# A mixture-of-experts block whose weights are laid out by the host in the order and shape in which the kernel loads them

## The chip, the cores and the metric

The kernel runs on one core of a Trainium2 chip. The metric is the device time of one execution in microseconds, the median of several runs. All data are float32. Weights lie in device memory (HBM) and are loaded into the on-chip memory SBUF (128 partitions) by DMA. The preparation of the inputs on the host is not part of the time.

## The reference

One layer over 256 tokens of width 1024. First an attention part with two branches, then a mixture of 32 experts of which each token uses four:

```
xn = rms_norm(h, attn_norm); proj = xn @ w_in            # 1024 x 4640
o_a = latent attention (8 heads), o_b = differential attention (4 heads)
merged = sigmoid(gate_a) * (o_a @ w_branch_mla) + sigmoid(gate_b) * (o_b @ w_branch_diff)
h = h + merged @ w_out
t = rms_norm(h, ffn_norm)
logits = t @ w_router + b_router; the best 4 per token, softmax over them
for e in range(32):
    u = t @ w1[e] + b1[e]                                # w1[e]: 1024 x 2048
    glu = minimum(u[:, :1024], 7); lin = clip(u[:, 1024:], -7, 7)
    a = glu * sigmoid(1.702 * glu) * (lin + 1)
    out = out + gates[:, e:e+1] * (a @ w2[e] + b2[e])    # w2[e]: 1024 x 1024
```

The expert weights are 32 x 12.6 MB = 402.7 MB, the head's weights (all that stands before the experts) about 29 MB.

## The kernel before

The program is written by hand, engine by engine: each engine has its own list of instructions, and semaphores tie them together. No scheduler changes the order.

Weights come in chunks of up to 128 x 2048 numbers (1 MB). The head has 28 chunks (table HEAD, line 91: matrix, first block of 128 rows, number of blocks, first column, columns). They go through eight places of a ring in SBUF. ACT and DVE split each into a high and a low part (split_hi, line 823, and split_lo), and PE multiplies the parts three times (split_part, line 432).

The experts are worked on in 16 pairs. A pair has 24 chunks (JOB_CHUNKS): 16 of the first layer (one block of 128 rows, for both experts, both the glu and the lin columns, one half of 512 columns each) and eight of the second layer (one block of 128 rows of both experts). PE takes up to 64 tokens of each of the two experts; each chunk is used for four products of 64 tokens by 512 columns (lines 749 and 761), and each product is two instructions, so the trace shows eight records of matmul a chunk. Between them PE gathers the tokens of the next pair by products with a 0/1 matrix (line 715) and scatters the results back (line 792). Further rounds run only if an expert has more than 64 tokens; the trace shows none.

The expert chunks go through a ring of 16 places (WIDE): 12 in the tile ring and four that lie in tiles whose head data are done with (latT_r, qka_r, v_r, lat_r). Four chunks of the first pair (ONCE) have places of their own, three of which ACT loads (lines 1017 and 1046). For all other chunks SP's queue waits until PE has used the chunk that held the place (ring_used, lines 329 to 347) and then issues the load. PE waits for a chunk by a count of its place's semaphore (arrive, line 430, and pair_arrive, lines 724 to 727). SP's loads are one list: first x, then head chunks with the small vectors between them (lines 297 to 319), then the expert chunks, of which two pairs (48 chunks) make one turn of the loop at line 352. An instruction that waits in SP's list holds back all loads behind it.

Each chunk is loaded by two DMA transfers. For an expert chunk, transfer a brings the half of expert 2 x pair + a (load_expert_chunk, line 253). In the first layer its source is, for each of 128 partitions, two rows of 512 numbers (2 KB each, the glu and the lin part); in the second layer it is one row of 1024 numbers (4 KB). A head chunk is split by its blocks of 128 rows, with rows of 288 to 1024 numbers. The gains and other small vectors come by 12 transfers (SMALL, lines 299 to 312), most of them one short row that is broadcast to 128 partitions.

Of the kernel before, what the change touches and what calls it, by code (L numbers as in the profile page):

```python
# [27 lines left out]
WA, WD = HA * VA, HD * DV  # L41
LAMBDA_INIT = 0.8 - 0.6 * math.exp(-0.3 * 0)

E, TOP_K, F = 32, 4, D
# [68 lines left out]
def lap_of(n):  # L113

    s = slot_of(n)
    if s >= WIDE:
        return 1
    return sum(slot_of(i) == s for i in range(min(n + 1, NHEAD))) + (0 if n < NHEAD else ring_place(n) // WIDE + 1)


def chunk_index(matrix, k, c0):
    return next(n for n, (w, k0, nk, c, _) in enumerate(HEAD) if (w, c) == (matrix, c0) and k0 <= k < k0 + nk)


def build(nc, x, attn_norm, w_in, q_lat_norm, kv_lat_norm, w_uq, w_ukv, q_norm, k_norm, dq_norm, dk_norm,
          lq1, lk1, lq2, lk2, subln, w_bmla, w_bdiff, w_out, ffn_norm, w_router, b_router,
          w1, b1, w2, b2, rope, out):
    ctx = ExitStack()
    with ctx:
        def sb(name, cols, dt=F32, parts=P):  # L130
            return ctx.enter_context(nc.sbuf_tensor(name, [parts, cols], dt))
# [3 lines left out]
        def sem(name):  # L135
            if name not in sems:
                sems[name] = ctx.enter_context(nc.semaphore(name))
            return sems[name]
# [54 lines left out]
        partial = sb("partial", SEQ)  # L193
        w_rt = sb("w_rt", KD * E)
        tab = sb("tab", NM * (ROPE_A + DD))
        g_qka, g_qkd = sb("g_qka", 2 * QK_A), sb("g_qkd", 2 * DD)
        g_sub, lam_in = sb("g_sub", DV), sb("lam_in", 4 * DD)
        b_rt = sb("b_rt", E)
        ident, before, ones = sb("ident", P), sb("before", P), sb("ones", P)
# [24 lines left out]

        matrices = {"w_in": w_in, "w_uq": w_uq, "w_ukv": w_ukv, "w_bd": w_bdiff, "w_ba": w_bmla, "w_out": w_out}
        landed = [sem(f"landed{s}") for s in range(WIDE + len(ONCE))]
# [7 lines left out]
        def slot(n, cols=SLOT):  # L234
            s = slot_of(n)
            return ring[:, s * SLOT:s * SLOT + cols] if s < RING else extra[s - RING]

        def head_view(n):
            _, _, nk, _, cols = HEAD[n]
            return v3(slot(n, nk * cols), nk)  # L240
# [8 lines left out]

        w1_v = w1.rearrange("e (k p) (g h n) -> e k p h g n", p=P, g=2, h=2)  # L250
        w2_v = w2.rearrange("e (k p) n -> e k p n", p=P)

        def load_expert_chunk(eng, n, c, pair):

            for a in range(2):
                if c < 2 * KD:

                    src = w1_v[2 * pair + a, c % KD, :, c // KD]
                    dst = slot(n).rearrange("p (e g n) -> p e g n", e=2, g=2)[:, a]
                else:  # L260
                    src = w2_v[2 * pair + a, c - 2 * KD]
                    dst = slot(n).rearrange("p (e n) -> p e n", e=2)[:, a]
                eng.dma_start(dst, src).then_inc(landed[slot_of(n)], 16)  # L263

        def gain(ap, n):
            return ap.rearrange("(a n) -> a n", a=1).broadcast_to([P, n])

        tab_v = tab[:].rearrange("p (m c) -> p m c", m=NM)

# [26 lines left out]
        def _(sp):  # L296
            sp.dma_start(acc[:, 0], x[0:P, :]).then_inc(sem("x_landed0"), 16)
            sp.dma_start(acc[:, 1], x[P:2 * P, :]).then_inc(sem("x_landed1"), 16)
            small = [(tab[:], rope), (g_qkd[:, 0:DD], gain(dq_norm, DD)), (g_qkd[:, DD:2 * DD], gain(dk_norm, DD)),
                     (g_qka[:, 0:QK_A], gain(q_norm, QK_A)), (g_qka[:, QK_A:2 * QK_A], gain(k_norm, QK_A)),  # L300
                     (lam_in[:, 0:DD], gain(lq1, DD)), (lam_in[:, DD:2 * DD], gain(lq2, DD)),
                     (lam_in[:, 2 * DD:3 * DD], gain(lk1, DD)), (lam_in[:, 3 * DD:4 * DD], gain(lk2, DD)),
                     (g_sub[:], gain(subln, DV)), (b_rt[:], gain(b_router, E)),
                     (v3(w_rt[:], KD), w_router.rearrange("(k p) n -> p k n", p=P))]
            assert len(small) == SMALL
            for n, (name, k0, nk, c0, cols) in enumerate(HEAD):
                if n == 4:
                    sp.dma_start(g_qlat, gain(q_lat_norm, Q_LORA)).then_inc(sem("lat_gain_landed"), 16)
                    sp.dma_start(g_kvlat, gain(kv_lat_norm, KV_LORA)).then_inc(sem("lat_gain_landed"), 16)
                if 6 <= n < 6 + SMALL // 2:  # L310
                    for dst, src in small[2 * (n - 6):2 * (n - 6) + 2]:
                        sp.dma_start(dst, src).then_inc(sem("small_landed"), 16)
                if n >= HEAD_RING:
                    sp.wait_ge(ring_used, n - HEAD_RING + 1)
                src = matrices[name].rearrange("(k p) n -> p k n", p=P)
                for a in range(2):
                    ks = slice(a * nk // 2, (a + 1) * nk // 2)
                    sp.dma_start(head_view(n)[:, ks, :], src[:, k0 + ks.start:k0 + ks.stop, c0:c0 + cols])\
                      .then_inc(landed[slot_of(n)], 16)

# [56 lines left out]
        def _(pool):  # L377
# [39 lines left out]
            for m in range(NM):  # L417
                pool.wait_ge(sem("ob_normed"), m + 1)
                pool.tensor_tensor(o_b[:, m], o_b[:, m], g_sub[:].unsqueeze(1).broadcast_to([P, HD, DV]), ALU.mult)\
                    .then_inc(sem("ob_ready"), 1)  # L420
# [3 lines left out]
        def _(pe):  # L424
# [3 lines left out]
            def arrive(n):  # L428

                pe.wait_ge(landed[slot_of(n)], 32 * lap_of(n))  # L430

# [241 lines left out]
            for h in range(2):  # L673
                turn_half(t_sb, h, sem("t_turned"), sem("hg_ready"))
            pe.wait_ge(sem("small_landed"), 16 * SMALL)
            wr = v3(w_rt[:], KD)
            for i in range(2):
# [43 lines left out]
            def pair_arrive(i, cycle, c):  # L721
                if isinstance(cycle, int):
                    n = NHEAD + i * JOB_CHUNKS + c
                    pe.wait_ge(landed[slot_of(n)], 32 * lap_of(n))
                else:
                    n = NHEAD + CYCLE + i * JOB_CHUNKS + c
                    pe.wait_ge(landed[slot_of(n)], 32 * (CYCLE // WIDE) * cycle + 32 * (lap_of(n) - CYCLE // WIDE))
                return slot(n)
# [83 lines left out]
        def _(act):  # L812
# [10 lines left out]
            def split_hi(i):  # L823

                n = SPLIT[i]
                act.wait_ge(landed[slot_of(n)], 32 * lap_of(n))
                if i >= BUFFERS:
                    act.wait_ge(ring_used, SPLIT[i - BUFFERS] + 1)
                _, _, nk, _, cols = HEAD[n]
                act.copy(split_views(i)[0], slot(n, nk * cols)).then_inc(sem("hi_ready"), 1)  # L830
# [261 lines left out]
        def _(dve):  # L1092
# [42 lines left out]

            dve.wait_ge(sem("small_landed"), 16 * SMALL)
            link(tt(scratch_m[:, 0:2 * DD], lam_in[:, 0:2 * DD], lam_in[:, 2 * DD:], ALU.mult))
# [73 lines left out]
            link(ts(lam[:, 5:6], lam[:, 4:5], -LAMBDA_INIT, None, ALU.add))  # L1211
            ts(g_sub[:], g_sub[:], 1.0 - LAMBDA_INIT, None, ALU.mult).then_inc(sem("sub_gain_scaled"), 1)
            pairs = o_raw.rearrange("p m (h a) d -> p m h a d", a=2)
# [81 lines left out]
            for m in range(NM):  # L1295
                stt(logit_v[:, m, 0:E], bank[1][:, m * E:(m + 1) * E], rstd[:, 54 + m:55 + m], b_rt[:],  # L1296
                    ALU.mult, ALU.add).then_inc(sem("logits_read"), 1)
# [112 lines left out]
TABLES = 5  # L1410
SMALL = 12


def rope_tables():

    cols = []
    for dim in (ROPE_A, DD):
# [6 lines left out]

_INS = ['x', 'attn_norm', 'w_in', 'mla_q_lat_norm', 'mla_kv_lat_norm', 'mla_w_uq', 'mla_w_ukv', 'mla_q_norm',
        'mla_k_norm', 'diff_q_norm', 'diff_k_norm', 'diff_lambda_q1', 'diff_lambda_k1', 'diff_lambda_q2',
        'diff_lambda_k2', 'diff_subln', 'w_branch_mla', 'w_branch_diff', 'w_out', 'ffn_norm', 'w_router',
        'b_router', 'w_mlp1', 'b_mlp1', 'w_mlp2', 'b_mlp2']

# [15 lines left out]
```

## Time and profile before

| What | Value |
|---|---|
| Median of 3 runs | 1259.32 us (1255.83 to 1260.06) |
| Span of the profiled execution (its own time is known only as this) | 1257.3 us |
| PE busy | 1134.1 us (90%) |
| DVE / ACT / POOL busy | 305.0 / 206.9 / 36.1 us |
| Read from HBM | 437.08 MB, 348 GB/s over the span |
| Granted TensorE clock, mean | 0.992 of full speed |

The profile comes from one execution. PE is TensorE's matmuls, PEld its weight loads, SPq and ACTq are the queues of the engines that issue DMA. In tables of stretches "DMA share" is the mean share of time in which the 16 DMA engines had a packet under way; packets overlap a little, so that it can pass 1. GB/s is what they moved. A packet is one contiguous row, or one of the small writes that count a semaphore. For a group of DMA issues the last number is the median time from issue to landing.

### The profile page before, as it was taken

Reading aid. Unit: us, or ns where it says so; the run is one execution under the profiler, and the core shown is the slowest. Engines: PE = TensorE matmul, PEld = TensorE weight load, DVE = VectorE, ACT = ScalarE, POOL = GpSimd, SP = SyncE. Lnnn points to the kernel's source line nnn. Section 1 sums busy time; section 2 is a strip of 40 time slices with the busy share of each in tenths; the row PEclk is TensorE's granted clock in tenths of the full one; section 3 lists DMA queues with packets and bytes.
Section 4 is the critical chain, followed back from the end, with each engine's and each line's share of the span. In section 5 each row is a group of like instructions: output and inputs, shape, how many; then the busy total and the mean of one; then the engine's idle time right before and its main releaser. Section 6 shows DMA issues by size and latency. Waiting matters only on the chain.

```text
span 1257.3 us, 14740 instructions
## 1 busy us (share of the span) xinstructions
PE 1134.1 (90%) x5144; PEld 506.6 (40%) x5144; DVE 305.0 (24%) x550; ACT 206.9 (16%) x352; POOL 36.1 (3%) x44
## 2 busy tenths in 40 slices
PE   6999999999999998988888888989797979797976
PEld 6867778534434342323232323232332323232422
DVE  4567657211120220202011120202020111111111
ACT  5646574300101010101010101010000000000000
POOL 1007110000000000000000000000000000000000
PEclk9999999899999999999999999999999999999998
DMA  9653259899999999999999999999999999999994
GB/s 350 217 179 123 101 166 347 328 336 393 394 391 397 391 397 390 398 389 385 386 400 383 380 377 402 384 384 373 401 386 395 360 400 384 399 355 390 391 395 162
DMA packets 196734, 438.83 MB, mean 349 GB/s; under 512 B 15873, under 2 KB 19329, under 8 KB 196641
## 3 DMA queue, kind: packets, MB, share of 16 engines
q1 hardware_dynamic: 194656, 433.59, 93.1%
q10 hardware_dynamic: 2016, 4.59, 1.1%
q8 instruction: 19, 0.31, 0.1%
q14 instruction: 43, 0.34, 0.1%
HBM read 437.08 MB, written 1.05 MB: 348 GB/s over the span
## 4 chain that ended last, share of the span: by engine, by line
PE 44%; SPq 36%; DMA 10%; issue 7%; ACT 1%; DVE 1%; ACTq 0%; DVEq 0%
SPq L263 36%; PE bank L443 11%; PE bank L749 10%; DMA ring<-in_w_mlp 9%; PE bank L761 9%; PE bank L715 3%; PE bank L792 2%; PE bank L426 2%; PE bank L668 2%; PE bank L499 1%; PE bank L535 1%; PE bank L510 1%; SPq L329 1%; DMA gate_r<-in_attn_norm 0%; PE bank L790 0%
## 5 line engine op out<-in xcount | busy, mean ns | idle before, releaser
L749 PE MATMUL bank<-ring,feat_r 128*64 128x512 f32 x1504 | 343.6, 598 | 38.9 <-DMA ring<-in_w_mlp 38.9
L749 PEld LDWEIGHTS bank<-ring,feat_r 128*64 128x64 f32 x1504 | 99.4, 136 | 273.7 <-issue 176.7
L761 PE MATMUL bank<-ring,soft_r 128*64 128x512 f32 x768 | 179.8, 600 | 29.2 <-DMA ring<-in_w_mlp 29.2
L1363 DVE TENSOR_SCALAR gate_r<-bank 128x512 f32<-128x512 f32 x32 | 22.1, 692 | 526.4 <-PE bank L749 526.4
L443 PE MATMUL bank<-ring_s,feat_s 128*128 128x512 f32 (+2 forms) x448 | 136.7, 387 | 2.5 <-DVE ring_s L1117 2.3
L761 PEld LDWEIGHTS bank<-ring,soft_r 128*64 128x64 f32 x768 | 49.8, 136 | 141.1 <-issue 79.5
L1063 ACT ACTIVATE gate_r<-gate_r 128x512 f32<-128x512 f32 x32 | 20.2, 630 | 422.7 <-DVE gate_r L1363 422.7
L443 PEld LDWEIGHTS bank<-ring_s,feat_s 128*128 128x128 f32 x448 | 81.5, 191 | 17.7 <-issue 5.2
L443 PE MATMUL bank<-ring_s 128*128 128x512 f32 (+2 forms) x224 | 85.0, 380 | 0.0
L1379 DVE COPY soft_r<-bank 128x512 f32<-128x512 f32 x16 | 11.1, 692 | 285.9 <-PE bank L761 285.9
L1067 ACT COPY soft_r<-bank 128x512 f32<-128x512 f32 x32 | 18.8, 586 | 337.5 <-PE bank L426 337.5
L1117 DVE TENSOR_TENSOR ring_s<-ring,ring_s 128x1024 fp32r<-128x1024 f32 (+2 forms) x56 | 67.1, 1231 | 28.1 <-ACT ring_s L830 28.1
L715 PEld LDWEIGHTS bank<-qkT_r,tok_r 128*128 128x128 f32 x544 | 64.1, 197 | 13.9 <-issue 13.0
L715 PE MATMUL bank<-qkT_r,tok_r 128*128 128x128 f32 x544 | 67.3, 284 | 0.8 <-DVE qkT_r L1327 0.8
L668 PE MATMUL bank<-qkT_r 32*128 32x512 f32 x128 | 65.1, 628 | 0.6 <-DVE logit L1296 0.6
L792 PE MATMUL bank<-soft_r,qkT_r 128*128 128x512 f32 x128 | 60.0, 608 | 0.0
L830 ACT CAST ring_s<-ring 128x2048 fp32r<-128x2048 f32 (+2 forms) x28 | 50.1, 1793 | 14.8 <-PE bank L443 13.9
L1384 DVE TENSOR_TENSOR acc_r<-bank,acc_r 128x512 f32<-128x512 f32 x64 | 44.3, 692 | 18.4 <-PE bank L792 18.4
L443 PEld LDWEIGHTS bank<-ring_s 128*128 128x128 f32 x224 | 42.5, 190 | 7.2
L749 PE MATMUL bank<-v_r,feat_r 128*64 128x512 f32 x128 | 30.8, 602 | 8.9 <-DMA v_r<-in_w_mlp 8.9
L749 PE MATMUL bank<-lat_r,feat_r 128*64 128x512 f32 x128 | 30.7, 601 | 8.5 <-DMA lat_r<-in_w_mlp 8.5
L668 PEld LDWEIGHTS bank<-qkT_r 32*128 32x128 f32 x128 | 21.6, 188 | 41.2 <-issue 34.5
(205 smaller groups left out, 744.1 us busy)
## 6 DMA issues: line engine op xcount, KB each, us to landing
ring<-in_w_mlp SPq DMA_DIRECT2D x568, 512.0 KB, 11.1
latT_r<-in_w_mlp SPq DMA_DIRECT2D x48, 512.0 KB, 10.8
qka_r<-in_w_mlp SPq DMA_DIRECT2D x48, 512.0 KB, 11.3
v_r<-in_w_mlp SPq DMA_DIRECT2D x48, 512.0 KB, 11.4
lat_r<-in_w_mlp SPq DMA_DIRECT2D x48, 512.0 KB, 11.7
ring<-in_w_in SPq DMA_DIRECT2D x28, 512.0 KB, 4.8
ring<-in_w_out SPq DMA_DIRECT2D x8, 512.0 KB, 4.2
ring<-in_w_in SPq DMA_DIRECT2D x8, 384.0 KB, 8.5
```

What stands on the lines that cost most here:

```text
L263: eng.dma_start(dst, src).then_inc(landed[slot_of(n)], 16)
L426: return pe.transpose(dst, src, ident[0:rows, 0:rows])
L443: mm = pe.matmul(banks[m][:, 0:cols], featT[left][:, first + k, m * P:(m + 1) * P], right[:, k - k0, :], start=(k == 0 and left == 0 and r ...
L668: pe.matmul(bank[2 * f + g][:], pick.rearrange("p e s -> p (e s)"), b1_sb[:, c0:c0 + HALF], start=True, stop=False, skip_group_check=True)
L715: mm = pe.matmul(bank[6 + k // 4][:, (k % 4) * P:(k % 4 + 1) * P], t_sb[:, m, k * P:(k + 1) * P], onehot[:, m].rearrange("p e s -> p (e s) ...
L749: mm = pe.matmul(b[e * SLOTS:(e + 1) * SLOTS, :], xT[:, k, e * SLOTS:(e + 1) * SLOTS], w[:, e, g, :], start=False, stop=(k == KD - 1), ski ...
L761: mm = pe.matmul(bank[4 + h][e * SLOTS:(e + 1) * SLOTS, :], aT[k // 4][:, k % 4, e * SLOTS:(e + 1) * SLOTS], w[:, e, h, :], start=(k == 0) ...
L792: pe.matmul(bank[2 * h + m][:], gatedT[:, m * P:(m + 1) * P], y_sb[:, h * HALF:(h + 1) * HALF], start=not second, stop=True, skip_group_ch ...
L830: act.copy(split_views(i)[0], slot(n, nk * cols)).then_inc(sem("hi_ready"), 1)
L1117: tt(lo[:, c], slot(n, nk * cols)[:, c], hi[:, c], ALU.subtract).then_inc(sem("lo_ready"), 1)
L1363: ts(glu[:, f], bank[2 * f][:], LIMIT, None, ALU.min).then_inc(sem(f"glu_ready{f}"), 1)
L1384: tt(a, bank[i][:], a, ALU.add).then_inc(sem("acc_added"), 1)
```

## The change

Before the launch the host now writes three new arrays, and the kernel takes these in place of the weight matrices and the small vectors:

- expert_w [16, 24, 128, 2048]: each expert chunk as it will lie in SBUF, so that a partition's part is one contiguous row of 8 KB and a chunk is 1 MB without gaps. One transfer loads it.
- head_w: the 28 head chunks one behind the other in the same manner; a partition's row has nk x cols numbers (1152 to 2048, that is 4.6 to 8 KB). One transfer each.
- rows [128, 1184]: the rotation tables, all small gains, the router's bias and its weights, already repeated for 128 partitions. One transfer of 128 rows of 4736 bytes, issued ahead of head chunk 6.

x, attn_norm, the two latent gains, ffn_norm and the expert biases are loaded as before. All waits for a chunk count 16 where they counted 32. Places, ring, waits for free places and all other instructions stay.

```
-            for a in range(2):
-                if c < 2 * KD:
-                    src = w1_v[2 * pair + a, c % KD, :, c // KD]
-                    dst = slot(n).rearrange("p (e g n) -> p e g n", e=2, g=2)[:, a]
-                else:
-                    src = w2_v[2 * pair + a, c - 2 * KD]
-                    dst = slot(n).rearrange("p (e n) -> p e n", e=2)[:, a]
-                eng.dma_start(dst, src).then_inc(landed[slot_of(n)], 16)
+            eng.dma_start(slot(n), expert_w[pair, c]).then_inc(landed[slot_of(n)], 16)
...
-                if 6 <= n < 6 + SMALL // 2:
-                    for dst, src in small[2 * (n - 6):2 * (n - 6) + 2]:
-                        sp.dma_start(dst, src).then_inc(sem("small_landed"), 16)
+                if n == 6:
+                    sp.dma_start(rows_sb[:], rows).then_inc(sem("small_landed"), 16)
                 if n >= HEAD_RING:
                     sp.wait_ge(ring_used, n - HEAD_RING + 1)
-                src = matrices[name].rearrange("(k p) n -> p k n", p=P)
-                for a in range(2):
-                    ks = slice(a * nk // 2, (a + 1) * nk // 2)
-                    sp.dma_start(head_view(n)[:, ks, :], src[:, k0 + ks.start:k0 + ks.stop, c0:c0 + cols])\
-                      .then_inc(landed[slot_of(n)], 16)
+                src = head_w[HEAD_AT[n]:HEAD_AT[n] + P * nk * cols].rearrange("(p n) -> p n", p=P)
+                sp.dma_start(slot(n, nk * cols), src).then_inc(landed[slot_of(n)], 16)
...
-                pe.wait_ge(landed[slot_of(n)], 32 * lap_of(n))
+                pe.wait_ge(landed[slot_of(n)], 16 * lap_of(n))
...
+def head_weights(by_name):
+    parts = []
+    for name, k0, nk, c0, cols in HEAD:
+        block = by_name[name][k0 * P:(k0 + nk) * P, c0:c0 + cols]
+        parts.append(block.reshape(nk, P, cols).transpose(1, 0, 2).reshape(-1))
+    return np.concatenate(parts)
...
+def expert_weights(w1, w2):
+    up = w1.reshape(PAIRS, 2, KD, P, 2, 2, HALF).transpose(0, 5, 2, 3, 1, 4, 6).reshape(PAIRS, 2 * KD, P, SLOT)
+    down = w2.reshape(PAIRS, 2, KD, P, D).transpose(0, 2, 3, 1, 4).reshape(PAIRS, KD, P, SLOT)
+    return np.concatenate([up, down], axis=1)
```

Only SP's and ACT's lists change. The first place is SP's queue in the head, around chunk 6 (names: destination tile, source array, shape of the transfer). Before:

```order
L318 DMA ring<-in_w_in 128x2x384 x8
L308 DMA gate_r<-in_mla_q_lat_norm 128x768
L309 DMA gate_r<-in_mla_kv_lat_norm 128x256
L318 DMA ring<-in_w_in 128x2x288 x4
L312 DMA tab<-in_rope 128x192
L312 DMA g_qkd<-in_diff_q_norm 128x64
L318 DMA ring<-in_w_in 128x2x512 x2
L312 DMA g_qkd<-in_diff_k_norm 128x64
L312 DMA g_qka<-in_mla_q_norm 128x96
L318 DMA ring<-in_w_in 128x2x512 x2
```

And now, for the same stretch of SP's queue and a little beyond:

```order
L282 DMA ring<-in_head_w 128x1536 x4
L275 DMA gate_r<-in_mla_q_lat_norm 128x768
L276 DMA gate_r<-in_mla_kv_lat_norm 128x256
L282 DMA ring<-in_head_w 128x1152 x2
L278 DMA rows_sb<-in_rows 128x1184
L282 DMA ring<-in_head_w 128x2048 x4
L282 DMA ring<-in_head_w 128x1536 x3
```

Two transfers a chunk have become one, and the small vectors, two of which stood ahead of each of chunks 6 to 11, all stand ahead of chunk 6.

The second place is SP's queue at the first pair of experts. Before:

```order
L263 DMA latT_r<-in_w_mlp 128x2x512 x2
L263 DMA qka_r<-in_w_mlp 128x2x512 x2
L263 DMA v_r<-in_w_mlp 128x2x512 x2
L263 DMA lat_r<-in_w_mlp 128x2x512 x2
L263 DMA ring<-in_w_mlp 128x2x512 x10
L263 DMA qkd_r<-in_w_mlp 128x2x512 x2
L263 DMA ring<-in_w_mlp 128x2x512 x6
L263 DMA ring<-in_w_mlp 128x1024 x8
```

And now:

```order
L237 DMA latT_r<-in_expert_w 128x2048
L237 DMA qka_r<-in_expert_w 128x2048
L237 DMA v_r<-in_expert_w 128x2048
L237 DMA lat_r<-in_expert_w 128x2048
L237 DMA ring<-in_expert_w 128x2048 x5
L237 DMA qkd_r<-in_expert_w 128x2048
L237 DMA ring<-in_expert_w 128x2048 x7
```

The order of places is the same; each chunk is one row of the list instead of two, and first- and second-layer chunks have the same shape (the last seven are three of the first layer and four of the second).

## Rows read from the trace of the kernel before

**Rows 1.** The page: busy time of TensorE, and DMA share in 40 slices.
```profile
PE 1134.1 (90%) x5144; PEld 506.6 (40%) x5144; DVE 305.0 (24%) x550; ACT 206.9 (16%) x352; POOL 36.1 (3%) x44
...
DMA  9653259899999999999999999999999999999994
```

**Rows 2.** Stretches (us): length, busy us and count by engine, PE clock, DMA share, GB/s.
```profile
302.00:1229.00 927.00, 829.61 (x3652) 291.29 (x3648) 142.99 (x261) 64.36 (x115) 0.00 (x0) 1.00 1.04 389
0.00:40.00 40.00, 30.04 (x168) 29.39 (x169) 19.92 (x24) 22.34 (x26) 3.82 (x22) 0.96 0.98 342
40.00:120.00 80.00, 80.00 (x350) 58.80 (x348) 51.22 (x71) 44.85 (x83) 17.43 (x11) 1.00 0.52 170
120.00:200.00 80.00, 76.53 (x418) 63.58 (x417) 53.46 (x100) 49.33 (x88) 14.84 (x12) 1.00 0.48 160
...
536.00:556.00 20.00, 17.36 (x74) 5.08 (x72) 2.67 (x4) 0.63 (x1) 0.00 (x0) 1.00 1.05 387
564.00:578.00 14.00, 10.71 (x48) 3.26 (x50) 2.80 (x5) 1.48 (x3) 0.00 (x0) 1.00 1.03 409
580.00:592.00 12.00, 11.45 (x65) 5.83 (x64) 0.69 (x1) 1.76 (x3) 0.00 (x0) 1.00 1.02 358
```

**Rows 3.** What SP's queue waited for, 302 to 1229 us: total, times, longest.
```profile
SPq L263 <- PE bank L749: 11.9, 9, 3.8
```

**Rows 4.** SP's queue in order of time: start, length (us), what.
```profile
301.88 2.52 SPq L263 DMA_DIRECT2D ring<-in_w_mlp  x4
```

**Rows 5.** PE in order of time: start, length, what, [idle before <- releaser].
```profile
348.94 1.12 PE L790 MATMUL bank<-qkT_r,weightT 32*128 32x512 f32 x2
...
357.36 1.98 PE L668 MATMUL bank<-qkT_r 32*128 32x512 f32 x4
...
411.92 1.98 PE L668 MATMUL bank<-qkT_r 32*128 32x512 f32 x4
...
488.52 1.94 PE L749 MATMUL bank<-ring,feat_r 128*64 128x512 f32 x8 [0.68 <-DMA ring<-in_w_mlp]
...
1229.07 1.94 PE L761 MATMUL bank<-ring,soft_r 128*64 128x512 f32 x8 [0.62 <-DMA ring<-in_w_mlp]
```

**Rows 6.** The chain that ended last: shares by engine, and pieces (start, us, what).
```profile
PE 44%; SPq 36%; DMA 10%; issue 7%; ACT 1%; DVE 1%; ACTq 0%; DVEq 0%
...
574.17 5.21 issue
...
627.07 14.32 DMA ring<-in_w_mlp
...
757.65 14.35 DMA ring<-in_w_mlp
```

**Rows 7.** DMA of 302 to 1229 us (queue, issues), and issues of 564 to 578 us.
```profile
q1 hardware_dynamic: 156569, 359.77, 103.6%
...
ring<-in_w_mlp SPq DMA_DIRECT2D x520, 512.0 KB, 11.2
...
ring<-in_w_mlp SPq DMA_DIRECT2D x8, 512.0 KB, 14.0
```

**Rows 8.** What PE waited for from 10 to 240 us, first of eight entries.
```profile
PE bank L560 <- ACT soft_r L951: 2.7, 4, 0.9
```

**Rows 9.** Line 263, 562 to 572 us: duration min/median/max in ns.
```profile
L263 SPq DMA_DIRECT2D ring<-in_w_mlp x9: 332/946/2748, 562.2 to 571.2; - x9
```

**Rows 10.** ACT and DVE in order of time, at three places.
```profile
33.03 1.90 ACT L830 CAST ring_s<-ring 128x2048 fp32r<-128x2048 f32 x1
...
43.48 0.28 DVE L1137 TENSOR_TENSOR scratch_m<-lam_in 128x128 f32<-128x128 f32 x1
...
210.26 3.72 ACT L830 CAST ring_s<-ring 128x2048 fp32r<-128x2048 f32 x2 [2.09 <-PE bank L443]
```

**Rows 11.** The page's DMA queues: packets, MB, share of 16 engines.
```profile
q1 hardware_dynamic: 194656, 433.59, 93.1%
...
q14 instruction: 43, 0.34, 0.1%
```

More of the change, by code:

```diff
@@ L118, in lap_of, with build @@
     return sum(slot_of(i) == s for i in range(min(n + 1, NHEAD))) + (0 if n < NHEAD else ring_place(n) // WIDE + 1)
+HEAD_AT = [P * sum(nk * cols for _, _, nk, _, cols in HEAD[:n]) for n in range(NHEAD)]
 def chunk_index(matrix, k, c0):
     return next(n for n, (w, k0, nk, c, _) in enumerate(HEAD) if (w, c) == (matrix, c0) and k0 <= k < k0 + nk)
-def build(nc, x, attn_norm, w_in, q_lat_norm, kv_lat_norm, w_uq, w_ukv, q_norm, k_norm, dq_norm, dk_norm,
-          lq1, lk1, lq2, lk2, subln, w_bmla, w_bdiff, w_out, ffn_norm, w_router, b_router,
-          w1, b1, w2, b2, rope, out):
+def build(nc, x, attn_norm, q_lat_norm, kv_lat_norm, ffn_norm, b1, b2, head_w, expert_w, rows, out):
     ctx = ExitStack()
@@ L193, in build @@
         partial = sb("partial", SEQ)
[L194 to L198, printed above, removed]
+        rows_sb = sb("rows_sb", sum(ROW_PARTS))
+        cuts = [sum(ROW_PARTS[:i]) for i in range(len(ROW_PARTS) + 1)]
+        tab, g_qkd, g_qka, lam_in, g_sub, b_rt, w_rt = (rows_sb[:, a:b] for a, b in zip(cuts, cuts[1:]))
         ident, before, ones = sb("ident", P), sb("before", P), sb("ones", P)
@@ L223, in build @@
         bank = [ctx.enter_context(nc.psum_tensor(f"bank{i}", [P, HALF], F32)) for i in range(8)]
-        matrices = {"w_in": w_in, "w_uq": w_uq, "w_ukv": w_ukv, "w_bd": w_bdiff, "w_ba": w_bmla, "w_out": w_out}
         landed = [sem(f"landed{s}") for s in range(WIDE + len(ONCE))]
@@ L248, in split_views @@
             return ring_s[:, hi:hi + nk * cols], ring_s[:, lo:lo + nk * cols]
-        w1_v = w1.rearrange("e (k p) (g h n) -> e k p h g n", p=P, g=2, h=2)
-        w2_v = w2.rearrange("e (k p) n -> e k p n", p=P)
         def load_expert_chunk(eng, n, c, pair):
-            for a in range(2):
-                if c < 2 * KD:
-                    src = w1_v[2 * pair + a, c % KD, :, c // KD]
-                    dst = slot(n).rearrange("p (e g n) -> p e g n", e=2, g=2)[:, a]
-                else:
-                    src = w2_v[2 * pair + a, c - 2 * KD]
-                    dst = slot(n).rearrange("p (e n) -> p e n", e=2)[:, a]
-                eng.dma_start(dst, src).then_inc(landed[slot_of(n)], 16)
+            eng.dma_start(slot(n), expert_w[pair, c]).then_inc(landed[slot_of(n)], 16)
         def gain(ap, n):
             return ap.rearrange("(a n) -> a n", a=1).broadcast_to([P, n])
-        tab_v = tab[:].rearrange("p (m c) -> p m c", m=NM)
+        tab_v = tab.rearrange("p (m c) -> p m c", m=NM)
         def norm_rotate(eng, name, qk, m, n, width, r, gains, rot, tab0, tmp):
@@ L298, in _ @@
             sp.dma_start(acc[:, 1], x[P:2 * P, :]).then_inc(sem("x_landed1"), 16)
[L299 to L306, printed above, removed]
+            for n, (_, _, nk, _, cols) in enumerate(HEAD):
                 if n == 4:
@@ L418, in _ @@
                 pool.wait_ge(sem("ob_normed"), m + 1)
-                pool.tensor_tensor(o_b[:, m], o_b[:, m], g_sub[:].unsqueeze(1).broadcast_to([P, HD, DV]), ALU.mult)\
+                pool.tensor_tensor(o_b[:, m], o_b[:, m], g_sub.unsqueeze(1).broadcast_to([P, HD, DV]), ALU.mult)\
                     .then_inc(sem("ob_ready"), 1)
@@ L674, in _ @@
                 turn_half(t_sb, h, sem("t_turned"), sem("hg_ready"))
-            pe.wait_ge(sem("small_landed"), 16 * SMALL)
-            wr = v3(w_rt[:], KD)
+            pe.wait_ge(sem("small_landed"), 16)
+            wr = v3(w_rt, KD)
             for i in range(2):
@@ L723, in pair_arrive @@
                     n = NHEAD + i * JOB_CHUNKS + c
-                    pe.wait_ge(landed[slot_of(n)], 32 * lap_of(n))
+                    pe.wait_ge(landed[slot_of(n)], 16 * lap_of(n))
                 else:
                     n = NHEAD + CYCLE + i * JOB_CHUNKS + c
-                    pe.wait_ge(landed[slot_of(n)], 32 * (CYCLE // WIDE) * cycle + 32 * (lap_of(n) - CYCLE // WIDE))
+                    pe.wait_ge(landed[slot_of(n)], 16 * (CYCLE // WIDE) * cycle + 16 * (lap_of(n) - CYCLE // WIDE))
                 return slot(n)
@@ L825, in split_hi @@
                 n = SPLIT[i]
-                act.wait_ge(landed[slot_of(n)], 32 * lap_of(n))
+                act.wait_ge(landed[slot_of(n)], 16 * lap_of(n))
                 if i >= BUFFERS:
@@ L1134, in _ @@
                 split_lo(i)
-            dve.wait_ge(sem("small_landed"), 16 * SMALL)
+            dve.wait_ge(sem("small_landed"), 16)
             link(tt(scratch_m[:, 0:2 * DD], lam_in[:, 0:2 * DD], lam_in[:, 2 * DD:], ALU.mult))
@@ L1211, in _ @@
             link(ts(lam[:, 5:6], lam[:, 4:5], -LAMBDA_INIT, None, ALU.add))
-            ts(g_sub[:], g_sub[:], 1.0 - LAMBDA_INIT, None, ALU.mult).then_inc(sem("sub_gain_scaled"), 1)
+            ts(g_sub, g_sub, 1.0 - LAMBDA_INIT, None, ALU.mult).then_inc(sem("sub_gain_scaled"), 1)
             pairs = o_raw.rearrange("p m (h a) d -> p m h a d", a=2)
@@ L1295, in _ @@
             for m in range(NM):
-                stt(logit_v[:, m, 0:E], bank[1][:, m * E:(m + 1) * E], rstd[:, 54 + m:55 + m], b_rt[:],
+                stt(logit_v[:, m, 0:E], bank[1][:, m * E:(m + 1) * E], rstd[:, 54 + m:55 + m], b_rt,
                     ALU.mult, ALU.add).then_inc(sem("logits_read"), 1)
@@ L1410 @@
 TABLES = 5
-SMALL = 12
+ROW_PARTS = (NM * (ROPE_A + DD), 2 * DD, 2 * QK_A, 4 * DD, DV, E, KD * E)
 def rope_tables():
@@ L1422, in rope_tables, with row_params @@
     return np.ascontiguousarray(tabs.reshape(NM, P, -1).transpose(1, 0, 2).reshape(P, -1))
[L1425 to L1428, printed above, removed]
+def head_weights(by_name):
[8 more added lines that the diff above has]
+    return np.concatenate([up, down], axis=1)
+def row_params(a):
+    rows = np.concatenate([a["diff_q_norm"], a["diff_k_norm"], a["mla_q_norm"], a["mla_k_norm"], a["diff_lambda_q1"],
+                           a["diff_lambda_q2"], a["diff_lambda_k1"], a["diff_lambda_k2"], a["diff_subln"], a["b_router"]])
+    w_rt = a["w_router"].reshape(KD, P, E).transpose(1, 0, 2).reshape(P, KD * E)
+    return np.ascontiguousarray(np.concatenate([rope_tables(), np.broadcast_to(rows, (P, rows.size)), w_rt], axis=1))
 def kernel(**inputs):
@@ L1435 @@
     nc = _bacc.Bacc("TRN2", target_bir_lowering=False, num_devices=1, dynamic_dma_scratch_size=1024)
-    arrays, args = {}, []
-    for name in _INS + ["rope"]:
-        a = rope_tables() if name == "rope" else np.ascontiguousarray(inputs[name])[0]
-        arrays[f"in_{name}"] = a
-        args.append(nc.dram_tensor(f"in_{name}", a.shape, F32, kind="ExternalInput").ap())
+    a = {name: np.ascontiguousarray(value)[0] for name, value in inputs.items()}
+    laid = {name: a[name] for name in ("x", "attn_norm", "mla_q_lat_norm", "mla_kv_lat_norm", "ffn_norm", "b_mlp1", "b_mlp2")}
+    laid["head_w"] = head_weights({"w_in": a["w_in"], "w_uq": a["mla_w_uq"], "w_ukv": a["mla_w_ukv"],
+                                   "w_bd": a["w_branch_diff"], "w_ba": a["w_branch_mla"], "w_out": a["w_out"]})
+    laid["expert_w"] = expert_weights(a["w_mlp1"], a["w_mlp2"])
+    laid["rows"] = row_params(a)
+    arrays = {f"in_{name}": value for name, value in laid.items()}
+    args = [nc.dram_tensor(f"in_{name}", value.shape, F32, kind="ExternalInput").ap() for name, value in laid.items()]
     out = nc.dram_tensor("out_h", [SEQ, D], F32, kind="ExternalOutput").ap()
```

## The prediction

> **What bounds the kernel now.** I read the page first: TensorE is busy 90% of the span, which looks like the bound, and the DMA row is at 9 in nearly every slice of the last three quarters [rows 1]. These two cannot be told apart by busy time, so I took the stretches next. From 302 us to 1229 us the DMA share is 1.04 and the core receives 389 GB/s, while PE has 829.6 busy in 927 us [rows 2]. The list of what SP's queue waited for shows no wait for a ring slot after 302 us: the 11.9 us there all lie at the start, the last one ends with the issue at 301.88 us [rows 3, 4]. So from 302 us SP always has a slot and the transfers alone set the pace at which weights come.
>
> PE's own order of time shows when it feels this. At 357.36 and at 411.92 us two successive pairs of experts begin (the L668 bias products), 54.56 us apart with PE never idle: this is PE's own price of 24 chunks, 2.273 us each [rows 5]. At 488.52 us the first wait for a chunk stands (0.68 us, ahead of a chunk's eight records). By then PE has eaten the lead that the ring held. From there to 1229.07 us each pair costs what its transfers cost. The chain of waits says the same: SP's queue holds 36% and DMA 10% of the span, together more than PE's 44% [rows 6].
>
> How fast do the transfers go? 359.77 MB in 927 us [rows 7] are 343.1 chunks of 1.0486 MB at 2.702 us. Behind the mean stand two speeds: a stretch with only first-layer chunks (536 to 556 us, rows of 2 KB at line 257) has 387 GB/s, one with only second-layer chunks (564 to 578 us, rows of 4 KB at line 261) 409 GB/s; and now and then a slow place (580 to 592 us: 358 GB/s) [rows 2]. Before 240 us it is different: from 40 to 200 us the DMA share is about a half and PE's list of waits to 240 us names no DMA at all, its longest entry is 2.7 us for ACT [rows 2, 8]. The head is set by PE and its helpers.
>
> **The large part: expert chunks as one transfer with 8 KB rows.** The diff lays each chunk out as it will lie in SBUF. Bytes stay the same, PE, DVE and ACT keep their instructions; only the rows get longer and SP issues 48 transfers where it issued 96 in each cycle of two pairs.
>
> A chunk of 1,048,576 bytes at 387 GB/s takes 2.710 us, at 409 GB/s 2.564 us. With 16 DMA engines a chunk is 32 rows of 2 KB for each of them, so 84.7 ns a row, or 16 rows of 4 KB, so 160.2 ns a row. A straight line through both: 75.5 ns per 2 KB and 9.2 ns per row whatever its length. A row of 8 KB is then 4 x 75.5 + 9.2 = 311.2 ns, eight of them 2.490 us a chunk (421 GB/s). This is an estimate, beyond the two measured points. Its bounds: if a row over 4 KB brings nothing more, 2.564 us; if the cost per row went to nothing, 8 x 302 ns = 2.416 us. I take the line, since both points lie on the side from which it is drawn and its last step is small (0.074 us).
>
> The Trainium skill speaks against this: "DMA: Bandwidth & Descriptors", section "Where 436 GB/s comes from", says that a load from HBM is held by the HBM side at about 358 GB/s and not by the fabric at 435. By that rule no row length could help and the time would stay. The trace does not agree: both steady stretches lie above 358 (387 and 409).
>
> The slow places: two parts of 2.710 and one of 2.564 us make 2.661 us, by 343.1 chunks 913.0 us, against 927 measured. The other 14.0 us are the slow places. The diff touches no reason for them that I can see, since the DMA share stays at 1.02 there: packets take longer, none are missing. I keep 14 us; bounds 0 and 28.
>
> The sum: 343.1 x 2.490 = 854.3, plus 14.0 is 868.3 us where 927 stood: 58.7 us less. The end behind it is unchanged: the chunk of 1229.07 us is the last that PE waits for, and what follows (gather, four chunks, scatter, stores) is PE's and takes 28.2 us to 1257.3 [rows 5].
>
> **What is late next.** A pair would take 24 x 2.490 + 1.0 = 60.7 us by transfers, 54.56 by PE: DMA still bounds. PE would finish its stretch at 357.4 + 14 x 54.56 = 1121 us, about 1130 with the end, if weights were free; nothing near. Between 349 and 357 us PE releases no slot (the scatter from L790 on, up to L668) [rows 5]. A faster queue gets ahead by three chunks there; the ring has 16 slots, and at 2.490 us the DMA brings 23 chunks from 302 to 359 us where PE takes 24, so SP stalls little. I put it at 0, at most one chunk, 2.5 us.
>
> **Fewer transfers by themselves.** A transfer lands 11.2 us after its issue, yet one lands every 1.35 us [rows 7]: some eight are under way, and the latency is hidden. The halved count saves SP's time, which was not missing: an unblocked issue takes a third of a microsecond (332 ns) [rows 9], the rest of its time SP is held back by its own full queue. At the end of a cycle SP stands still for 5.21 us [rows 6]; the 14.0 us from issue to landing in that stretch [rows 7] cover it, and afterwards longer ones will. I cost the count at 0, bounds 0 to 3 us of gain.
>
> The Trainium skill ("DMA: Bandwidth & Descriptors", section "Anatomy of one DMA — SWDGE (gpsimd) path") gives each DMA a fixed 2.0 us. If that added up, the 343 transfers saved would be 686 us. The trace does not agree for queued transfers: 1.35 us for the whole of one is less than that fixed part alone.
>
> **The head.** 56 transfers of head chunks become 28 with rows of 4.6 to 8 KB, and 12 small ones become one of 128 x 4736 bytes (0.606 MB) that now stands whole ahead of chunk 6. Its price: 0.606 MB at 342 GB/s [rows 2] is 1.8 us before chunk 6 lands. In front of that chunk lie about 7 MB (x, gains, chunks 0 to 5, the new array), with it 8 MB: about 23.5 us at 342 GB/s. ACT casts chunk 6 at 33.03 us [rows 10]: 9 us to spare. The lambda vectors are first read at 43.48 us [rows 10]. PE waits for none of this [rows 8]. ACT issues three expert chunks rather than six halves; the cast behind the first four waited 2.09 us for PE anyway [rows 10]. Head: 0, bounds -2 to +2 us.
>
> **Result of the sum.** 1257.3 - 58.7 = 1198.6 us of span. The median of the runs is 1259.3, 2.0 us above the profiled span, within the 4.2 us over which three runs spread. I add it: 1201 us. A change under 0.3% (3.8 us) counts as none.
>
> **Rivals.**
> *The gain ends at 4 KB rows* (15%). SP might cut rows, or the second layer may be quick for another reason, such as its unbroken 512 KB source. For it: no row in the trace shows 8 KB in this queue. Against: the cost per row has no reason to stop. Then 343.1 x 2.564 + 14.0 = 893.6: 33.4 us less, 1226 us.
> *Nothing changes* (5%). The memory side hands out 387 to 389 GB/s on the average, whatever the rows, and 409 is its mood after a slow place. Against: the same two numbers come back in each pair. 1259 us. It would also be the case where the layout of rows does not reach the packets.
> *Long rows are slow on an engine* (5%), so the time is longer. The place is one DMA engine's handling of one 8 KB row. The instruction queue fetches in packets of this kind: 43 packets, 0.34 MB, 0.1% of 16 engines' span [rows 11], that is 20.1 us or 468 ns each (234 to 702 by the rounding). Eight rows of 468 ns are 3.74 us a chunk, and 343.1 x (3.74 - 2.66) would be 371 us more, 1630 us. The point from which it decides is 8 x t above 2.661 us, 333 ns a row. Against: such a fetch shares the engine with the stream, so its time holds other packets.
> *Faster still* (5%). 2.416 us a chunk and no slow places: 828.9 us, 98 us less, 1161 us. PE would stay just behind (2.273).
>
> **How the numbers follow.** The forecast, 70%: 1201 us, its own range 1184 to 1217 (slow places 0 to 28 us, head 2). The second case at 1226 is taken in with its spread to 1238; the low end 1180 takes some of the fast case. Chances: faster 0.90 (0.70 + 0.15 + 0.05), within 0.3% 0.05, slower 0.05.
>
> **What the profile after would show.** GB/s near 421 in every slice from 302 us on, the same in first- and second-layer stretches; packets in SP's queue down from 194,656 [rows 11] to about 61,000 (384 x 128 rows of expert chunks, 28 x 128 of the head, 16 small ones for each of some 430 transfers; over 110,000 if rows are cut at 4 KB). PE's first wait for a chunk comes later than 488 us: its lead shrinks by 2.531 - 2.273 = 0.26 us a chunk rather than 0.43, which puts it near 560 us. Two pairs take about 121.5 us where they took 130.6 (two equal pieces of the chain, at 627.07 and 757.65 us [rows 6]). Issue to landing grows to 25 us or more, and the head ends where it did. The prediction is wrong if the rate stays below 412 GB/s, if SP starts to wait for slots in the long stretch (then PE would be the bound), or if the pairs begin later than at 244.8 us.

## The result and the profile after

| What | Before | After |
|---|---|---|
| Median of 4 runs each | 1258.34 us | 1177.08 us (1176.03 to 1179.89) |
| Ratio | | 0.9365, 95% interval 0.9346 to 0.9383 |
| Span of the profiled execution | 1257.3 us | 1174.1 us |

The change saves 81 us; the prediction was 1201 us with a range down to 1180. The direction was right and the size too small by 24 us.

The page of the kernel after, part 1 and the 40 slices of part 2 (DMA share in tenths, GB/s), for comparison with [rows 1]:

```profile
PE 1116.0 (95%) x5144; PEld 510.5 (43%) x5144; DVE 305.0 (26%) x550; ACT 206.8 (18%) x352; POOL 36.1 (3%) x44
...
DMA  9654238889999999999999999999999999999995
GB/s 370 224 192 142 73 108 334 347 323 422 389 421 419 421 421 421 422 422 421 422 422 423 422 422 421 423 421 422 422 422 422 422 422 422 422 421 422 422 422 208
```

From the twelfth slice to the last but one, every slice has 419 to 423 GB/s. The kernel before had values from 355 to 402 in the same row of its page. Stretches after, columns as in [rows 2]:

```profile
302.00:1146.00 844.00, 811.90 (x3640) 296.07 (x3635) 143.00 (x261) 64.28 (x115) 0.00 (x0) 1.00 1.01 422
536.00:556.00 20.00, 20.00 (x96) 6.79 (x96) 3.66 (x7) 1.22 (x2) 0.00 (x0) 1.00 1.01 422
564.00:578.00 14.00, 14.00 (x54) 4.80 (x52) 4.35 (x9) 0.58 (x1) 0.00 (x0) 1.00 1.01 421
580.00:592.00 12.00, 12.00 (x54) 3.93 (x52) 2.67 (x4) 0.63 (x1) 0.00 (x0) 1.00 1.01 421
```

387, 409 and 358 GB/s [rows 2] have all become 421 or 422: the two speeds are gone, and so is the slow place. PE's first wait for a chunk in the long stretch, and the last, answer to [rows 5] (PE in order of time):

```profile
609.16 1.94 PE L724 MATMUL bank<-ring,soft_r 128*64 128x512 f32 x8 [0.52 <-DMA ring<-in_expert_w]
...
1146.07 1.94 PE L724 MATMUL bank<-ring,soft_r 128*64 128x512 f32 x8 [0.57 <-DMA ring<-in_expert_w]
```

The first comes at 609 us (488 before), the last at 1146.07 us, 28.0 us before the end (28.2 before). Two equal pieces of the chain of waits (start, length, what) stand 119.28 us apart, where it was 130.6 [rows 6]; that is 48 chunks at 2.485 us and nothing else:

```profile
642.28 26.47 DMA ring<-in_expert_w
761.56 26.48 DMA ring<-in_expert_w
```

The page's queues (packets, MB, share), and one group of DMA issues of 302 to 1146 us (count, KB each, us to landing), answer to [rows 7, 11]:

```profile
q1 hardware_dynamic: 60768, 433.56, 90.3%
...
q14 instruction: 10, 0.08, 0.0%
```
```profile
ring<-in_expert_w SPq DMA_DIRECT2D x258, 1024.0 KB, 26.2
```

SP's queue has 60,768 packets, so rows of 8 KB are moved whole. A transfer now lands 26.2 us after its issue, with one landing every 2.485 us: some ten are under way. The line that I read past is the last one of the page: the packets with which instructions are fetched fell from 43 [rows 11] to 10. SP now waits for free places (302 to 1146 us, as [rows 3]):

```profile
SPq L237 <- PE bank L712: 116.0, 70, 11.6
SPq L237 <- PE bank L724: 47.9, 28, 5.1
```

I had named such waits as a sign that PE is the bound. It is not: the share is 1.01 and PE waits for chunks from 609 us on. SP waits while the ten transfers that it has issued last are still under way, and the DMA engines never run dry.

### The profile page after: what moved, and what is told of

Its sections match the earlier page's. It is cut to its first block, busy times and chain, and to the rows that moved or that the text cites. A ratio compares the mean times of both kernels' runs of the same rounds, so it can differ in the third digit from the quotient of the medians.

```text
span 1174.1 us, 13641 instructions
## 1 busy us (share of the span) xinstructions
PE 1116.0 (95%) x5144; PEld 510.5 (43%) x5144; DVE 305.0 (26%) x550; ACT 206.8 (18%) x352; POOL 36.1 (3%) x44
## 3 DMA queue, kind: packets, MB, share of 16 engines
q1 hardware_dynamic: 60768, 433.56, 90.3%
## 4 chain that ended last, share of the span: by engine, by line
PE 45%; SPq 38%; DMA 12%; issue 3%; ACT 1%; DVE 1%; ACTq 0%; DVEq 0%
SPq L237 37%; PE bank L712 13%; PE bank L406 12%; DMA ring<-in_expert_w 11%; PE bank L724 8%; PE bank L678 2%; PE bank L389 2%; PE bank L755 2%; PE bank L631 2%; PE bank L462 1%; PE bank L498 1%; PE bank L473 1%; SPq L292 1%; DMA gate_r<-in_attn_norm 0%; PE bank L753 0%
## 5 line engine op out<-in xcount | busy, mean ns | idle before, releaser
L712 PE MATMUL bank<-ring,feat_r 128*64 128x512 f32 x1504 | 336.3, 596 | 8.6 <-DMA ring<-in_expert_w 8.6
L712 PEld LDWEIGHTS bank<-ring,feat_r 128*64 128x64 f32 x1504 | 102.5, 137 | 232.7 <-issue 200.3
L724 PE MATMUL bank<-ring,soft_r 128*64 128x512 f32 x768 | 177.4, 599 | 15.3 <-DMA ring<-in_expert_w 15.3
L1347 DVE TENSOR_TENSOR acc_r<-bank,acc_r 128x512 f32<-128x512 f32 x64 | 44.3, 692 | 18.5 <-PE bank L755 18.5
L755 PEld LDWEIGHTS bank<-soft_r,qkT_r 128*128 128x128 f32 x128 | 22.7, 189 | 36.7 <-issue 36.7
L1015 ACT COPY feat_r<-bank 128x512 f32<-128x512 f32 x34 | 19.9, 585 | 78.6 <-PE bank L678 78.6
## 6 DMA issues: line engine op xcount, KB each, us to landing
ring<-in_expert_w SPq DMA_DIRECT2D x284, 1024.0 KB, 26.2
```

The costliest lines, as they stand in the source:

```text
L712: mm = pe.matmul(b[e * SLOTS:(e + 1) * SLOTS, :], xT[:, k, e * SLOTS:(e + 1) * SLOTS], w[:, e, g, :], start=False, stop=(k == KD - 1), ski ...
L724: mm = pe.matmul(bank[4 + h][e * SLOTS:(e + 1) * SLOTS, :], aT[k // 4][:, k % 4, e * SLOTS:(e + 1) * SLOTS], w[:, e, h, :], start=(k == 0) ...
L755: pe.matmul(bank[2 * h + m][:], gatedT[:, m * P:(m + 1) * P], y_sb[:, h * HALF:(h + 1) * HALF], start=not second, stop=True, skip_group_ch ...
L1347: tt(a, bank[i][:], a, ALU.add).then_inc(sem("acc_added"), 1)
```

## Experiments

Thirteen more kernels ran, and each is told here. Ratios are against the kernel before on the same chip. Where a chunk comes by two transfers, the waits for it count 32 as in the kernel before.

**One transfer, 2 KB rows.** Rows and count of transfers taken apart: the host cuts each chunk into four blocks of 128 x 512.

```
-            eng.dma_start(slot(n), expert_w[pair, c]).then_inc(landed[slot_of(n)], 16)
+            eng.dma_start(slot(n).rearrange("p (q n) -> p q n", q=4), expert_w[pair, c].rearrange("q p n -> p q n"))\
+                .then_inc(landed[slot_of(n)], 16)
```

> Experts laid out as [4, 128, 512] blocks: still one 1 MB transfer a chunk, but rows of 2 KB (source contiguous in 256 KB blocks). Row theory (time is set by the rows a DMA engine handles): 2.710 us a chunk, 387 GB/s, the stretch of 339.7 chunks 76 us longer than with 8 KB rows, run near 1253 us, or 1267 if the slow places (14 us) belong to 2 KB rows. Rival, the number of transfers: SP's list is as short as in the changed kernel, so 1177 us. Rival for the slow places, the length of SP's loop (instructions fetched anew at each turn): none here, GB/s even at 387.

Measured: 1257.29 us, ratio 0.9981 (0.9964 to 0.9998), 386 or 387 GB/s in every slice from the tenth to the last but one, 10 instruction packets. One transfer a chunk is worth nothing against the rows; but there are no slow places, though all rows are short.

**Two transfers, 2 KB rows.** The same layout, the transfer cut into two of two blocks each.

> The same 2 KB rows and blocks, but two 512 KB transfers a chunk as before the change, so SP's loop is long again. Row theory: within 0.5% of the run with one transfer. If the slow places come from SP's long loop they stand here (once in two pairs, at the loop's turn, 14 us in all) and not in the run with one transfer; if they come from 2 KB rows they stand in both; if they come from the old source layout (2 KB pieces 4 KB apart) in neither.

Measured: 1276.22 us, ratio 1.0131 (1.0099 to 1.0164), 18.9 us over one transfer; 42 instruction packets. The slow places are there, once in a turn of SP's loop. In the chain of waits SP stands still for 5.66 us at the loop's turn, and as it ends the stream drops (stretches, columns as above):

```profile
583.52 5.66 issue
```
```profile
584.00:588.00 4.00, 4.00 (x35) 3.56 (x32) 0.00 (x0) 0.59 (x1) 0.00 (x0) 1.00 1.04 380
588.00:592.00 4.00, 3.89 (x21) 1.17 (x19) 0.00 (x0) 0.59 (x1) 0.00 (x0) 1.00 0.55 202
592.00:596.00 4.00, 2.63 (x12) 0.80 (x14) 0.00 (x0) 0.00 (x0) 0.00 (x0) 1.00 0.98 321
```

So not rows and not the old layout. Left are the count of transfers and the length of SP's list, 96 loads with their register work.

**One transfer, 4 KB rows, and two transfers, 4 KB rows.** Blocks of 128 x 1024 (q=2 in the lines above).

> Blocks of [2, 128, 1024], one transfer a chunk, rows of 4 KB throughout. Row theory: 160.2 ns a row, 2.564 us a chunk, 409 GB/s, 27 us more than with 8 KB rows, 1204 us; 1218 if the slow places belong to short rows. If the time goes with the number of transfers: 1177 us.

> Rows of 4 KB throughout as in the run of 1202 us, but two transfers of 512 KB a chunk. If two transfers cost 19 us whatever the rows (as between the 2 KB runs): 1221 us. If the 19 us belong to 2 KB rows in two transfers: 1202 to 1206 us.

Measured: 1202.02 us, ratio 0.9548 (0.9520 to 0.9576), 410 GB/s; with two transfers 1224.54 us, ratio 0.9738 (0.9721 to 0.9755). The row theory holds to 2 us, and two transfers cost 22.5 us here too (24 us by the two ratios).

**Two transfers of 64 partitions, 8 KB rows.** Meant to keep the long rows and double the count.

```
+            for a in range(2):
+                h = slice(a * P // 2, (a + 1) * P // 2)
+                eng.dma_start(slot(n)[h, :], expert_w[pair, c, h]).then_inc(landed[slot_of(n)], 16)
```

> Rows of 8 KB, but two transfers of 64 partitions a chunk: 96 transfers in SP's loop as before the change. Row theory: 1177 us, 422 GB/s. Number of transfers: back near 1258 us. Long loop makes slow places: 14 us more, 1191 us, with dips once in two pairs.

Measured: 1830 and 1836 us in two executions, 1867 and 1966 in the two others, none of what was expected. One stretch:

```profile
302.00:1120.00 818.00, 563.90 (x2094) 175.91 (x2090) 85.56 (x169) 36.95 (x66) 0.00 (x0) 0.90 1.02 263
```

The DMA engines are busy as ever (1.02) and move 263 GB/s: a row of 8 KB takes 0.53 us in this stretch of the trace (median), where it takes 0.31 us in the changed kernel. Why a transfer of 64 partitions has slow rows stays open. The run says nothing on the count of transfers. The Trainium skill ("DMA: Bandwidth & Descriptors", section "Rules for kernel authors") advises against two transfers to disjoint halves of the partitions, since they serialize. This case agrees with the advice, but the price is more than standing in line: 1830 us is 55% above 1177.

**A longer list for the same transfers.** The changed kernel (8 KB rows, 48 loads a turn) with waits that are already met ahead of each load in the loops (PAD of them, 8 and then 24); and 8 with 2 KB rows.

```
+                        for _ in range(PAD):
+                            sp.wait_ge(sem("x_landed0"), 16)
```

> The changed kernel with 8 waits that are already met put ahead of each chunk's load in SP's loops: the same 48 transfers of 8 KB rows a turn, but a list of instructions as long as with 96 transfers. Long-list theory (slow places come when SP's loop is too long to be held and is fetched anew at each turn): instruction packets up from 10 to about 40, SP stands still for some 5 us at the loop's turn. If the fetching itself slows the stream: slow places again, 1190 us. If they need a shallow queue or many transfers, none: the 26 us of queued loads cover the stop, 1177 us.

> The same padding on the kernel with one transfer of 2 KB rows a chunk (1257 us). Long-list theory: slow places as with two transfers, 1270 to 1276 us. Number-of-transfers theory: stays at 1257.

> 24 waits that are already met ahead of each chunk's load in SP's loops where the run of 1199.7 us had 8: 98 KB more of instructions in two loops against the changed kernel (then 24.6 KB more: 48 instructions of 64 bytes for each wait added), the same 48 transfers and the same seven turns. Theory A, one DMA engine carries the fetches of instructions besides its sixteenth of the weights, and what is lost is in proportion to the fetches: some 11 fetches a turn rather than 5, a loss of 22.7 x 11 / 5 = 50 us, 1227 us, and near the end the stream again runs on one engine alone (DMA share 0.06), for longer or with waits earlier on. Theory B, the turn of the loop costs a fixed stop of some 3 us: as before, 1200 us.

Measured: 1199.74 us (ratio 0.9545, 0.9525 to 0.9564), 1276.70 us (1.0156, 1.0136 to 1.0177) and 1214.65 us (0.9642, 0.9626 to 0.9659). Two of these waits make one instruction: with 24 waits the trace has 4032 more instructions than the changed kernel, 576 a turn. At the 64 bytes of the expectation that is 37 KB in the loop that runs, and 74 KB with the loop for further rounds, which does not run; the expectation had 98 KB. Instruction packets:

| Kernel | Packets | Time | Without the long list | us per packet more |
|---|---|---|---|---|
| 8 KB, 8 waits | 42 | 1199.74 | 1177.08 (10 packets) | 0.71 |
| 8 KB, 24 waits | 63 | 1214.65 | 1177.08 (10) | 0.71 |
| 2 KB, 8 waits | 42 | 1276.70 | 1257.29 (10) | 0.61 |
| 2 KB, two transfers | 42 | 1276.22 | 1257.29 (10) | 0.59 |
| 4 KB, two transfers | 42 | 1224.54 | 1202.02 (10) | 0.70 |

Taken from the ratios, each against the kernel before on its own chip, the five prices are 0.71, 0.66, 0.69, 0.59 and 0.75. The two for 8 KB rows agree within the intervals, so the loss goes with the packets fetched and not with the turn: a fixed cost a turn is refuted (1200 was expected, 1215 measured). The 1227 us of the other theory were off since a turn fetches 7.6 packets and not 11. Where the loss sits shows at the end of the stream. The padded kernel (8 waits), then the changed kernel:

```profile
1138.00:1154.00 16.00, 14.91 (x64) 4.23 (x60) 2.67 (x4) 0.63 (x1) 0.00 (x0) 1.00 1.01 415
1164.00:1180.00 16.00, 14.42 (x84) 7.00 (x84) 2.80 (x5) 2.66 (x5) 0.00 (x0) 1.00 0.06 27
```
```profile
1140.00:1156.00 16.00, 14.34 (x82) 6.85 (x80) 2.80 (x5) 2.66 (x5) 0.00 (x0) 1.00 1.01 420
```

An empty queue after SP's stop is not the reason: the padded kernel has 26 us of loads queued where the padded one with 2 KB rows has some 14, and it loses as much. A share of 0.06 is one engine of 16, and 27 GB/s is one sixteenth of 422: for some 18 us a single DMA engine has weights left while 15 have finished.

The packet records of this trace show how it fell behind. Each of the 31 fetches between 400 us and the end of the stream takes 0.31 to 0.32 us. A row of weights starts as the fetch ends (within 0.004 us) and takes 0.72 to 0.73 us, where such a row takes 0.31. One fetch thus takes 0.31 + 0.41 = 0.72 us from the stream of the engine that carries it, and the table has 0.71 us a packet. Over the 32 fetches that the padding added that is 23 us, and the loss is 22.7: so they all weigh on the same engine, as it would be a sixteenth of this if they were spread. That is inferred from count, share and time: no view names the engine of a packet.

With 26 us of queued loads the other 15 run ahead, and most of the debt falls due at the end. With short rows the queue is shallow (11 us with two transfers of 2 KB rows) and they stop for the late engine in each turn (share 0.55 above). In the packet records of the kernel with two transfers of 2 KB rows one engine works alone for a microsecond before 723.5 us, and at the end of the stream for some 4 us only. SP's stop falls in the same place there, and no run with short rows parts the two. For the kernel before, the count of fetches and the 18 us below fit the same price, but its slow place looks different: the share stays at 1.02 [rows 2], and single rows of 2 KB take up to 2.2 us there. How a fetch leads to such rows stays open. The Trainium skill ("DMA: Bandwidth & Descriptors", section "Queues, rings and completion order") has each DMA engine take turns between its queues, the one for instruction refill among them; the trace agrees, with a row of weights that follows each fetch without a gap.

**No turn of the loop.** Two transfers of 2 KB rows, and the kernel before itself, with SP's loop over the pairs written out (flat=True keeps the waits that the loop's loads have).

```
-            with sp.Fori(1, PAIRS // 2) as j:
+            for j in range(1, PAIRS // 2):
                 for i in range(2):
-                    load_pair(i, 2 * j + i, j)
+                    load_pair(i, 2 * j + i, j, flat=True)
```

> Two transfers of 2 KB rows a chunk (1276 us with SP's loop), but SP's loop over the pairs written out as a straight list: no turn of a loop, each instruction fetched once, ahead of need. If the slow places come from the turn (stop of 5 us, then issues one behind the other without a pause): none, 1257 us. If they come from fetching: spread over the whole stretch, 1276 us. If from the number of transfers: 1276 us too, with no more instruction packets than now.

> The kernel before with nothing changed but SP's loop over the pairs, written out as a straight list: old layout, old head, 2 and 4 KB rows, two transfers. If the change's gain is rows (61.8 us) plus the shorter list (19.5 us): 1258.3 - 19.5 = 1239 us, instruction packets down from 43 to under 20. If the slow places of the kernel before belong to its source layout: 1258 us.

Measured: 1257.03 us (ratio 0.9988, 0.9976 to 1.0000) with 14 packets, equal to one transfer; and 1240.95 us (ratio 0.9860, 0.9843 to 0.9878) with 15 packets. Writing out SP's loop alone gives the kernel before 18 us, with its layout untouched. Its stretches, to be set beside [rows 2]:

```profile
536.00:556.00 20.00, 16.64 (x70) 4.66 (x68) 2.67 (x4) 0.63 (x1) 0.00 (x0) 1.00 1.05 387
564.00:578.00 14.00, 12.12 (x62) 4.83 (x63) 2.79 (x5) 1.49 (x3) 0.00 (x0) 1.00 1.03 409
580.00:592.00 12.00, 12.00 (x44) 4.19 (x44) 3.92 (x8) 1.16 (x2) 0.00 (x0) 1.00 1.05 389
```

The two speeds of the rows stay, the slow place (358) is gone. At 28 packets fewer, 18.5 us are 0.66 us a packet.

**Head and experts apart.** Each part of the change alone, the other as before.

> Only the head and the small vectors changed, experts as before (two transfers, 2 and 4 KB rows). My prediction held the head at 0 (-2 to +2 us): 1256 to 1260 us. The trace of the changed kernel has the first expert product 2.9 us earlier; if that is the head's loads, the run is 1255 us with that product near 242 us. If the slow places came from the head's part of the change, they are gone: 1241 us.

> Only the experts changed, the head and the 12 small transfers as before. Row theory: 1177 to 1180 us, 422 GB/s without slow places, first expert product near 244.8 us. If the head's part gave the 24 us that the prediction missed: 1201 us.

Measured: head alone 1258.31 us, ratio 0.9997 (0.9985 to 1.0009); experts alone 1177.76 us, ratio 0.9358 (0.9342 to 0.9374). The head is worth nothing that can be measured. The first expert product of the profile after stands at 241.94 us (244.75 us before), but with the new head alone at 245.79 us and with the new experts alone at 245.91 us; neither part alone brings the 3 us, and one profiled execution of each does not tell more.

**16 KB rows.** Two neighbouring chunks as one 2 MB transfer where their places adjoin.

```
+                eng.dma_start(ring[:, s * SLOT:(s + 2) * SLOT], expert_w[pair, c // 2].rearrange("p a n -> p (a n)"))\
+                    .then_inc(doubled[(ring_place(n) % WIDE - EXTRA) // 2], 16)
```

> From the second pair on, two neighbouring chunks that share two neighbouring places of the ring are one 2 MB transfer with rows of 16 KB (12 chunks of 16; the four in other tiles stay single). By the straight line a 16 KB row takes 613 ns, 2.453 us a chunk (427 GB/s) against 2.490: 0.75 x 335 x 0.037 = 9 us less, 1168 us. Rivals: rows over 8 KB are cut into 8 KB, time as with 8 KB (1177); or long rows are slow on an engine, over 1190. A place is now free one chunk later, which could make the loads wait: also above 1177.

Measured: 1172.65 us, ratio 0.9325 (0.9307 to 0.9342), against 0.9358 (0.9342 to 0.9374) for the new experts: 5.1 us less, the fastest kernel here. Its stretch:

```profile
320.00:1120.00 800.00, 772.15 (x3484) 291.65 (x3480) 136.62 (x251) 62.43 (x112) 0.00 (x0) 0.99 1.01 426
```

Three parts of 2.453 and one of 2.490 us make 426 GB/s, as the line has it. Of the 9 us expected 5 came. From the measured 2.485 us a chunk it would have been 8; where the rest went was not tried (a place must be free one chunk longer).

## Why the prediction was wrong in size

1. **Long rows: right.** The line gave 2.490 us a chunk, measured 2.485 (422 GB/s). Over all four lengths it holds: 387, 410, 422 GB/s, and 426 with three quarters at 16 KB. Of the time it was to bring 58.7 us; from the kernel before with the straight list (1240.95) to the new experts (1177.76) it is 63 us. Of these 343.1 x (2.661 - 2.485) = 60 are rows, and 3 are the five packets fewer (15 to 10). The rivals that ended at 4 KB rows (1226), with no change, or with slow long rows are refuted; the kernel with 4 KB rows, at 1202, shows what the first would have given.
2. **The slow places: wrong, and this is the failed step.** I wrote that the diff touches no reason for them, since the DMA share stays at 1.02, and kept 14.0 us. Their reason was SP's loop of 96 loads, whose instructions were fetched anew in each turn by an engine that also carries weights: the same kernel with that loop written out loses the slow places and 18 us. The change halves the list, fetches fall from 43 packets to 10, and the slow places go. The 14.0 us were themselves too low against these 18, so that even my bound of 0 for them ended at 1184 us and not at 1177. The rival that was faster still had "no slow places" in it, but tied to rows without any cost of their own and with 5% only. The share of 1.02 told me that the engines were busy, and nothing of why.
3. **Fewer transfers gain nothing by themselves: right as stated, wrong in what it left out.** Two transfers with a straight list equal one (1257.03 and 1257.29). But I counted SP's time and the latency only, both covered, and not the instructions that come with each load. The 5.21 us stop at the turn [rows 6] was in my hand; I asked only whether the queue covers it, not why SP stops. The 2.0 us a DMA that I quoted from the Trainium skill ("DMA: Bandwidth & Descriptors", section "Anatomy of one DMA — SWDGE (gpsimd) path") stand there for DMAs issued from GpSimd; the loads here are issued from SP, so they put that figure to no test.
4. **Sum.** 63 us for rows and 18 us for the list are the 81 us measured. The prediction had 58.7 of the first and none of the second: 23 of the 24 us by which it missed. The last one is the median before, 1258.3 us in the result and 1259.3 in the prediction.
5. **Head and small vectors: right**, 0.
6. **What is late next: right.** PE's first wait was to come near 560 us and came at 609, since without slow places the gap is 0.21 us a chunk. The sign that I named for PE as bound (waits for places) was wrong: SP was to stall 2.5 us at most, it waits 164 us in all, and the stream loses nothing by it.
7. **The price of a fetch: misread.** I took 468 ns a packet from the page's rounded share, for the rival of slow long rows. The packet records of the kernel before have 0.31 to 0.34 us from 400 us on, as for a row of 8 KB. I then priced a fetch only as a row like others, and not what it does to the engine that carries it.

## What to carry to other kernels

Where DMA is the bound, fit a line through the rates of two row lengths in the trace: it gave 8 KB and 16 KB rows within 1%. Look at the page's count of instruction packets for each loop that a queue engine runs: if it grows with the turns, the loop's body is fetched anew each time, and here each packet cost 0.6 to 0.75 us of the weight stream; a shorter body or a straight list took that away at no cost. The slow places came once in a turn and had their reason in the loop, so the first question on a periodic loss is whose period it is.

## What the runs showed of the hardware that was not expected

- A fetch of 8 KB of instructions takes 0.31 us, and the row of weights behind it 0.72 us in place of 0.31 (31 of 31 fetches in the padded kernel).
- A single DMA engine that falls behind holds back a whole stream: each transfer has landed only at a count of 16, one from each. With a deep queue little of the loss is seen in the rates (417 to 423 GB/s in most slices of the padded kernel), and most falls due at the end, at 27 GB/s and a share of 0.06.
- Two transfers of 64 partitions with 8 KB rows moved 263 GB/s at a share of 1.02, against 422 for one of 128 partitions: 1830 us rather than 1177.
- The cost of a row beyond its bytes, 9.2 ns for an engine, is the same from 2 to 16 KB.
